# A two-block transformer layer on one core: the residual on the vector engine alone, four tiles wide into the first up stage, two norms read later, matmuls on constants inside two waits, and other bank waits at out2 and up2

## What is computed

```python
def first_block(x, ...):                      # D_MODEL 2048, SEQ 256, D_FF 5632
    h = rmsnorm(x, pre_mix_g)
    proj = h @ w_in                           # two kinds of attention, 16 heads each
    ...
    mix = jnp.concatenate([o_a, o_b], axis=-1) @ w_out
    x = x + rmsnorm(mix, post_mix_g)
    h = rmsnorm(x, pre_ffn_g)
    u = causal_dwconv(h @ w_up, conv_w, conv_b)
    gate, val = jnp.split(u, 2, axis=-1)
    y = (jax.nn.gelu(gate, approximate=True) * val) @ w_down
    return x + rmsnorm(y, post_ffn_g)

def second_block(x, ...):                     # 20 heads of 128, D_FF_2 8192
    h = rms_norm(x, g_mix)
    ...                                       # attention, two gated branches
    x = x + mixed @ w_out
    h2 = rms_norm(x, g_mlp)
    return x + jnp.square(jax.nn.relu(h2 @ w_up)) @ w_down
```

## Time and profile before

| | us |
|---|---|
| median of 3 runs | 2632.62 (2628.98 to 2632.97) |
| the profiled execution | 2629.61 |
| its span, first to last instruction | 2627.9 |
| PE busy | 2557.3 |
| DVE busy | 1788.0 |
| ACT busy | 1288.9 |
| POOL busy | 280.6 |

### The profile page before, as it was taken

The page is one execution under the profiler, slowest core; times in us unless marked ns, Lnnn a source line. Parts: engine busy times, 40 slices in busy tenths (PEclk is TensorE's granted clock), DMA queues, the critical chain, the costliest instruction groups (busy, mean ns, idle before and its releaser), DMA issues.

```text
span 2627.9 us, 44360 instructions
## 1 busy us (share of the span) xinstructions
PE 2557.3 (97%) x14612; PEld 2248.6 (86%) x14612; DVE 1788.0 (68%) x2904; ACT 1288.9 (49%) x2374; POOL 280.6 (11%) x303
## 2 busy tenths in 40 slices
PE   7999979999999999979999999999999999999999
PEld 6888768888888888869999998887888888888888
DVE  7777779875886788666655566667666565665664
ACT  6565545444444444446555565555544444444443
POOL 1000134320330133130000000000100000000000
PEclk9999989999999999989999999999999999999999
DMA  6444445555555555536555545556555555555554
GB/s 225 143 144 145 145 143 161 191 170 192 182 186 180 190 182 189 185 98 203 173 174 172 177 138 181 185 187 204 184 184 185 184 187 185 187 186 185 187 186 137
DMA packets 163249, 461.42 MB, mean 176 GB/s; under 512 B 17962, under 2 KB 37310, under 8 KB 163134
## 3 DMA queue, kind: packets, MB, share of 16 engines
q1 hardware_dynamic: 163134, 459.91, 53.4%
HBM read 457.71 MB, written 2.13 MB: 175 GB/s over the span
## 4 chain that ended last, share of the span: by engine, by line
PE 88%; DVE 6%; ACT 3%; issue 2%; DMA 1%; POOL 0%; SPq 0%; POOLq 0%; DVEq 0%; ACTq 0%
PE G L655 77%; PE SB L655 9%; DVE wlo L1271 1%; PE MB L655 1%; DVE wlo L1264 1%; DVE x L438 1%; PE SB L844 1%; ACT y L1068 1%; DVE hS L1639 1%; DMA raw<-in_in 0%; ACT whi L996 0%; DMA raw<-in_out 0%; DMA x<-in_xT 0%; ACT hS L1201 0%; DVE y L437 0%
## 5 line engine op out<-in xcount | busy, mean ns | idle before, releaser
L655 PE MATMUL G<-hS,whi 128*128 128x512 f32 x3712 | 1311.6, 400 | 29.9 <-DVE wlo L1271 13.0
L655 PE MATMUL G<-hS,wlo 128*128 128x256 f32 x3712 | 1006.9, 281 | 0.0
L1271 DVE TENSOR_TENSOR wlo<-raw,whi 128x1024 fp32r<-128x1024 f32 (+3 forms) x790 | 903.4, 1184 | 92.6 <-ACT whi L996 77.3
L655 PEld LDWEIGHTS G<-hS,whi 128*128 128x128 f32 x3712 | 688.5, 189 | 186.2 <-DVE wlo L1271 14.9
L996 ACT ACTIVATE whi<-raw 128x1024 fp32r<-128x1024 f32 (+3 forms) x790 | 752.1, 998 | 74.7 <-DMA raw<-in_mix 28.9
L655 PEld LDWEIGHTS G<-hS,wlo 128*128 128x128 f32 x3712 | 703.3, 189 | 20.4
L655 PE MATMUL G<-aS,whi 128*128 128x512 f32 x1952 | 685.0, 400 | 2.5 <-DVE og L1337 2.3
L1049 ACT ACTIVATE tmp<-G 128x256 f32<-128x256 f32 x374 | 143.2, 383 | 953.2 <-PE G L655 952.5
L655 PE MATMUL G<-aS,wlo 128*128 128x256 f32 x1952 | 527.8, 282 | 6.9 <-DVE aS L462 4.6
L655 PEld LDWEIGHTS G<-aS,whi 128*128 128x128 f32 x1952 | 359.6, 189 | 82.0 <-DVE og L1337 3.5
L655 PEld LDWEIGHTS G<-aS,wlo 128*128 128x128 f32 x1952 | 369.8, 189 | 21.4 <-DVE aS L462 5.5
(11 more groups left out here) (168 smaller groups left out, 1882.0 us busy)
## 6 DMA issues: line engine op xcount, KB each, us to landing
raw<-in_up SPq DMA_DIRECT2D x304, 512.0 KB, 4.7
raw<-in_dn SPq DMA_DIRECT2D x160, 512.0 KB, 4.6
raw<-in_in SPq DMA_DIRECT2D x192, 256.0 KB, 3.4
raw<-in_in SPq DMA_DIRECT2D x64, 512.0 KB, 4.7
raw<-in_out SPq DMA_DIRECT2D x64, 512.0 KB, 4.9
raw<-in_dn SPq DMA_DIRECT2D x64, 448.0 KB, 4.0
raw<-in_mix SPq DMA_DIRECT2D x64, 384.0 KB, 3.1
raw<-in_mix SPq DMA_DIRECT2D x64, 320.0 KB, 3.3
```

Source lines behind the costliest of these rows:

```text
L655: return pe.matmul(o, w, m, start=start, stop=stop, skip_group_check=False)
L1271: dve.tensor_tensor(wlo[:, slot, a * P:b * P], raw[:, h0 % RAW_SLOTS, 0:(b - a) * P], whi[:, slot, a * P:b * P].bitcast(F32), ALU.subtract ...
```

## The change

Line numbers below are those of the changed kernel where they differ.

- **Residual.** DVE does it all, in nine groups: tiles 0, 1, and seven pairs. The multiply reads the spread norm from the PSUM bank `SB1`, and ACT's copy to `rsb` is gone for norms 3 and 5. The low parts of a group come after the next group's two steps.
- **Folds.** All five are on DVE, also in `pre`.
- **Constant matmuls.** `idle_work` issues 4, 2 and 5 matmuls of two constants, 128x256, into `SB3`: inside `norm_sums` for norms 3 and 5, after it, and after `norm_spread`.
- **Unit 3.** The fourth unit's splits of `up1_0` and `in2` stand before the residual on ACT and DVE; its slot is given free by the first sum of the norm. In `in2` units 4 and 5 stand before the folds.
- **Four wide.** `up1_0` starts four output tiles together for input tiles 0 to 10, then finishes them one after another; they are read out into four buffers `upb`. The first two iterations are written out (`UP_FIRST`); norm 4 is summed and spread in the second one.
- **Norm 6** is summed at half of `in2`'s second head, and the first head's steps come four positions later.
- **Bank waits.** At `out2`, tiles 0 and 1 wait only for `mix2`'s gate tiles, and tile 0 is read out before unit 3 is split; at `up2_0` the wide start waits for all but the last tile of `out2`.
- **dn1_2.** Its step Y2 comes in its own iteration, before tile 3.

```diff
-WIDE = 3
+WIDE = {"up1_0": 4, "up2_0": 3}
+TOGETHER = 11
+NORM6 = 12
+LATE = 4
...
+        upb = sb("upb", [P, 4, T])
...
+        FILL_IN = {3: (4, 2, 5), 5: (4, 2, 5)}
...
-        RESIDUAL = {0: (1, "dve"), 1: (4, "dve"), 4: (8, "pool"), 8: (12, "dve"), 12: (16, "pool")}
+        RESIDUAL = ((0, 1), (1, 2), (2, 4), (4, 6), (6, 8), (8, 10), (10, 12), (12, 14), (14, 16))
...
-            r = rsb[:, 0:1, :].to_broadcast([P, b - t, T])
+            r = SB[1][:, 0:T].unsqueeze(1).to_broadcast([P, b - a, T])
             chain(eng.tensor_tensor(y[:, tiles, :], y[:, tiles, :], r, ALU.mult))
             chain(eng.tensor_tensor(x[:, tiles, :], x[:, tiles, :], y[:, tiles, :], ALU.add))
...
+        UP_FIRST = ((),
+                    ("X0@0", "X1@0", "X2@0", "X3@0", "F0@0"),
+                    ("F1@0", "F2@0", "G0@0", "M1@0", "X0@1"),
+                    ("F3@0", "G2@0", "M3@0", "X1@1", "F0@1", "X2@1", "F1@1", "G0@1"))
...
+            def idle_work(n):
+
+                for _ in range(n):
+                    mm(SB[3][:, 0:T], ident, cs[:, 0:T], True, True)
...
+                if st.name == "out2" and isinstance(it, int) and it == 0 and p < 2:
+
+                    f = ST["out2"].g(0, 0) - 2
...
+                    if st.name == "up1_0" and isinstance(it, int) and it == 1 and (p, kk) in ((0, 4), (1, 1)):
+                        (norm_sums if p == 0 else norm_spread)(NORM_IN[st.name])
...
-                    if w0(i - 1):
-
-                        dve.wait_ge(u_scaled, i - 1)
-                    add_to(sq[:, p % 2 * T:(p % 2 + 1) * T])
+                    if w0(i - 3):
+
+                        dve.wait_ge(u_scaled, i - 3)
+                    add_to(upb[:, p, :])
...
-                        pool.wait_ge(ncopy, n)
-                        pool.wait_ge(yg, KT * (n // 2 - 1))
-                        c = Chain(pool, res_pool, 4, n // 2 - 2)
-                        for t in (4, 12):
-                            residual(pool, c, t)
-                    if n != 7:
-                        fold(pool, n, 0, 2)
```

More of the change, by code:

```diff
@@ L393, in splits_when @@
                 return "later"
+            if isinstance(it, int) and it == 0 and (st.name, p) == ("out2", 0):
+                return "after"
             if isinstance(it, int) and it == 0 and (st.name, p) in (("out1", 0), ("out1", 1), ("out1", 2), ("mix2", 2)):
                 return "later" if (st.name, p) == ("out1", 0) else "after"
-            return "after" if is_wide(st, it) and p == WIDE - 1 or st.name == "pre" and p else "before"
+            return "after" if is_wide(st, it) and p == WIDE[st.name] - 1 or st.name == "pre" and p else "before"
         def input_of(st, p):
@@ L524, in run_stage @@
             lo = 0
-            if wraps or n == 1 or st.name == "mix2":
+            if st.name == "up1_0":
+                for it in range(2):
+                    for p in range(st.nm):
+                        for name in UP_FIRST[p] if it else ():
+                            step(name[:2], int(name[3]))
+                        mtile(st, it, p, False)
+                lo = 2
+            elif wraps or n == 1 or st.name == "mix2":
                 body(0, True, n == 1)
@@ L745, in mtile @@
                         end.then_inc(mt_done, 1)
-                    if kk == 0 and p == WIDE if is_wide(st, it) and k < W_SLOTS else within == 0 and (st.prev or k):
+                    if within == 0 and (st.prev or k):
                         one.then_inc(unit_used, 1)
@@ L1032, in mtile @@
                 when = splits_when(st, it, p, last)
-                if when == "before":
+                if when == "before" and not (st.name == "up1_0" and isinstance(it, int) and it == 0 and p == 0):
                     splits(st, it, p, last)
                 carried(1, st, it, p + 0.5, step)
-                if st.name in NORM_IN and isinstance(it, int) and it == 0 and p == (1 if st.wide else 2):
+                if st.name == "up1_0" and isinstance(it, int) and it == 1 and p == 1:
+                    spread(NORM_IN[st.name])
+                if st.name in NORM_IN and st.name != "up1_0" and isinstance(it, int) and it == 0 and p == (1 if st.wide else 2):
                     spread(NORM_IN[st.name])
@@ L1234, in _ @@
             for st in stages:
-                for n in NORM_BEFORE.get(st.name, ()):
-                    norm(n)
+                if st.name in ("up1_0", "in2"):
+                    split(st, 0, AHEAD)
                 if st.name in ("pre", "up1_0", "in2"):
@@ L1309, in mtile @@
                 first = st.name in NORM_IN and isinstance(it, int) and it == 0
-                if when == "before" and not (first and (p == 1 or p == 0 and st.name == "pre")):
+                if when == "before" and not (first and (p == 1 or p == 0 and st.name in ("pre", "up1_0", "in2"))):
                     splits(st, it, p, last)
@@ L1316, in mtile @@
                 if first and p == 0:
-                    norm(NORM_IN[st.name])
-                    splits(st, it, 0 if st.name == "pre" else 1, last)
+                    if st.name != "up1_0":
+                        norm(NORM_IN[st.name])
+                        splits(st, it, 0 if st.name == "pre" else 1, last)
                 if st.name == "mix2" and last and p in EARLY_TILES:
@@ L1323, in mtile @@
                 read_out(st, it, p)
+                if st.name == "up1_0" and first and p == 1:
+                    fold(dve, NORM_IN[st.name], 3, 5)
+                if st.name == "up1_0" and first and p == 3:
+                    norm(NORM_IN[st.name])
                 if when == "after":
@@ L1684, in _ @@
                     if st.name == "in2":
-                        look_ahead(st, 0, 0)
-                    fold(dve, n, 2, 5)
+                        look_ahead(st, 0, 1)
+                        look_ahead(st, 0, 2)
+                    if st.name == "up1_0":
+                        fold(dve, n, 0, 3)
+                        split(st, 0, AHEAD + 1)
+                    else:
+                        fold(dve, n, 0, 5)
                 if st.name == "out2":
```

149 lines of the change are left out of this document (86 added, 63 removed).

## The result

The changed kernel takes **2608.88 us**, the median of 4 runs (2604.37 to 2609.40); the kernel before, run beside it, 2632.16 (2628.98 to 2632.97). The ratio is **0.9912**, 95% interval 0.9899 to 0.9924: 23 us less. The forecast was 2614.0. The profiled execution took 2608.7 us, with a span of 2607.1 (2627.9 before).

What follows compares the result with a forecast made beforehand. PE, busy 97% of the span, was taken as the bound. Gains of 13.9 + 1.4 + 1.4 + 1.0 + 0.9 = 18.6 us took the profiled 2629.6 to 2611.0, median 2614.0; range 2603 to 2626.

Steps and rivals of the forecast that it cites:

- part 4: Entry of `up1_0`: tenth tile begins 3.0 us earlier, net gain 1.4 us after a clock loss; bounds -2 to 11.
- part 6: Small gains: 1.0 us at `up2_0`, no longer waiting for the last read-out, and about 0.9 us in `pre`.
- Part 3: Following input tiles at `in2`: DVE sets the pace, head 0 done 15.8 us earlier; net gain 13.9 us, bounds 10 to 15.
- the 1.9 given back: At `in2`, what reduces the 15.8 us gain to 13.9, including head 1's 1.4 us wait for unit 4.
- the signs of being wrong: Multiply from PSUM over 1 us, clock 0.50 after the spreads, or head 1 of `in2` waiting for weights.
- the wait for norm 4: At `up1_0`, PE waits 4.7 us before its seventh tile, as ACT copies the norm behind splits of units 6 to 8.
- the second rival: At `up1_0`, the late norm costs nothing, as loads or ACT's copy come sooner: 2604.1 us; chance 0.12.
- the 1.7 us that were assumed: At `up1_0`, one clock loss after an isolated wait: 3.4 us at half speed, up to 1.7 us lost.
- Part 5: At `out2`, the wait before tile 2 goes and tile 3 begins 1.4 us earlier; bounds 0 to 3.
- The clock rival: Clock still falls to half at the entries of `up1_0` and `in2`, costing 12.6 us: 2626.6 us; chance 0.13.
- The slow add as another thing's doing: DVE's residual add is slow without POOL too, in all 18 groups at two entries: 2650 us; chance 0.04.
- nothing is gained: Whole kernel: POOL's part was hidden and DVE has more work; within 5 us of before, 2630 us; chance 0.05.

Runs made afterwards that it cites:

- in2_unit3_late: Changed kernel with the splits of unit 3 of `in2` moved back behind the residual on ACT and DVE; ratio to the kernel before 0.9930.
- before_res_dve: Kernel before, with only the residual and all folds of norms 4 and 6 on DVE, in the old tile groups; ratio 0.9970.
- pool_busy: Changed kernel plus six GpSimd multiplies on constants, which nobody waits for, during the residual of `in2`; ratio to the kernel before 0.9947.
- no_constants: Changed kernel without its 22 constant matmuls; ratio to the kernel before 0.9918.
- copy_early: Changed kernel with ACT's copy of norm 4 in `up1_0` ahead of unit 8's splits; ratio to the kernel before 0.9910.
- after_again: Changed kernel run once more, unedited, as yardstick for other runs; ratio to the kernel before 0.9911.

## Why the prediction was right, point by point

The time lies 5 us under the forecast, 0.2%; the interval given held it. In the pieces 18.6 us were predicted and 20.8 measured: 2.6 more in part 4 and 2.1 at `dn1_0`, 2.4 less in part 6. These misses cancel in part, which is luck.

- **Part 3, in2**, the term that carries the sum: 13.9 predicted, 13.9 measured. Its main reasons stand: the length of a multiply with an operand in PSUM (0.68 for 0.69 to 0.73), DVE's time from the first low part's end to the last one's (16.1 us for 16.5), and unit 3, whose return costs more than the 2.90 in the sum (in2_unit3_late). Two steps inside it were off. The last four low parts come in one burst, faster than the 1.04 us that PE needs for a tile, and head 1 begins 3.2 us after them and not 1.1:

```profile
1166.81 1.68 DVE L1696 SCALAR_TENSOR_TENSOR hS<-x,pv,hS 128x256 fp32r<-128x256 f32 x4
...
1171.68 0.33 PE L681 MATMUL SB<-whi,hS 128*128 128x384 f32 x1
```

  So the gain up to there is 14.0 us, not 15.8. In return the wait of 1.4 us for unit 4, part of the 1.9 given back, did not come; the text had it in the sum and, against that, among the signs of being wrong. With it the sum has head 1 begin 21.4 us behind the end of the spread, and it was 21.6: the later end of head 0 took the place of the wait. That the two agree to 0.1 us in the end is luck. GpSimd as the cause of the slow add is shown both ways, by taking it away (before_res_dve) and by putting it back (pool_busy).
- **Part 4, up1_0**: 1.4 predicted, 4.0 measured. The step that was mis-sized is the wait for norm 4. The last half unit was put 43.0 us behind the start of the spread (421.5 less 378.52); it was there after 40.2 (420.35 less 380.12). The loads began where they were put (406.79, 26.7 us behind the spread; forecast 26.8). Six of 2.46 us from 405.3 end at 420.1, so the 421.5 holds 1.4 us more that the text does not name; and the 2.46 is from the mean rate of a stretch in which the loads also paused. All six were there 13.6 us after the first issue, 2.26 us each: of the second rival, the part that was right. The wait was 2.46 us and not 4.7, and the tenth tile began 5.2 us earlier, not 3.0. Of the 5.2 the clock took back the 1.7 us that were assumed (0.86 over the 12 us from 440), and the wait at `dn1_0` gave 0.4. First tile (3.5 us behind the end of the spread, predicted 3.6) and four tiles (24.0, predicted 23.7) were right.
- **Part 5 and up2_0**: 2.4 predicted, 2.3 measured, in the places named.
- **Part 6, pre**: 0.9 of gain predicted, 1.5 of loss measured. The norm did come 0.8 earlier (29.72 for 30.55). Two steps failed: that all of this reaches the end of the stage, and that nothing else changes there. ACT waited longer for the loads of `in1`:

```profile
50.36 1.06 ACT L1049 ACTIVATE whi<-raw 128x1024 fp32r<-128x1024 f32 x1 [2.10 <-DMA raw<-in_in]
```

  Before, this split stood at 50.26: at 50 us both kernels are level. PE came to its wait for the bias rows 0.6 us earlier and left it at 63.09, where the kernel before left it at 62.98:

```profile
63.09 1.22 PE L681 MATMUL SB<-heads 64*128 64x128 f32 x4 [2.73 <-DVE heads L1535]
```

  This profile was a late one. In the ten of the changed kernel and its variants without constants in that wait, the wait ends at 61.76 to 63.24, on average 0.5 us earlier than in the two kernels without the change (62.98 and 62.96). The other 1.4 us of the loss come behind it, from the clock: 0.50 for 6.8 us, where it was 3.4 before. The four profiles that had 3.4 too began `out1` 0.4 to 1.4 us earlier than before (277.06 to 278.04, for 278.46). At equal clock the term is a gain of about the size predicted, and the clock's swing hides it.
- **dn1_0 to norm 5**: 0 predicted, 2.1 measured. Before, the clock fell at `dn1_0` (0.79) behind a wait of 1.97; now, behind 1.60, it stays at 1.00 in all profiles of the changed code. Which edit shortened that wait wasn't tried; before_res_dve gains 1.3 here with the wait still 1.93, so it is in part luck.
- **The clock rival** had a true mechanism and a wrong price: no_constants brings the half clock back, for 6.8 and 10.2 us and not 17 each, and costs 1.8 us, not 12.6. In the prediction this rival had a chance of 0.13 and set the upper end of the range; it should have been worth less of both. Of the rule that each long wait is paid again by a cold start (the Trainium skill, "TensorE: Matmul & The Clock Gate", section "HAM oscillation — how this bites in real kernels"), whose example has waits of 3 to 5 us, the runs show what the trace before did, agreement in part: 3.24 was paid, 3.13 in copy_early was not; and of shorter ones 2.46 went by without, while in after_again 2.77 and 2.30 both were paid.
- **The slow add as another thing's doing** and **nothing is gained** fell with the rows of DVE.

## What to carry to other kernels

The add that took nearly six times its usual length was held up by another engine: look at what runs beside such an instruction before giving that neighbour more work, and look whether one operand can come from PSUM. When input comes faster, ask which weights are next; here the faster residual alone was worth 3 us at `in2`, the whole change 14, and 5.5 of these hang on the fourth unit's split. And split the span at fixed matmuls, and look up the clock in each piece: where it does not change, most pieces agree within 0.5 us (`in1` within 1.0) and tell what runs of one kernel that differ by 5 us hide.

## What the runs showed of the hardware

- GpSimd holds the vector engine up by the kind of operand: beside GpSimd's multiply, 1.67 us for an add of 128x512 with two SBUF operands (0.69 alone), 0.68 for the multiply with one of them in PSUM (0.68 alone). All three are from pool_busy.
- The same program at the same place had the tensor engine's clock at 0.77, 0.89 and (in two sister programs) 1.00 over 15 us, behind waits of 2.73, 1.96, 2.09 and 1.86 us. From the second scores to `out1` the swing is 3.3 us, more than most single edits here are worth.
- The half clock cost most where the tensor engine set the pace: 3.3 us between the scores and `out1` for 6.8 us of it, and 0.9 us at `in2` for 10.2.
